# Retention's output matrix in column-block pairs, with four weight quads of each pair as seven block products

## The reference, cut to what matters

```python
y = (normalised_heads * silu(g)).reshape(B, S, R_HEADS * R_V_DIM) @ ret_w_out
x = layer_norm(ALPHA * x + y, ln_gain[i], ln_bias[i])
```

## Time and profile before

| | |
|---|---|
| median of 3 runs | 2163.74 us (2163.69 to 2163.83) |
| the profiled execution | 2162.95 us |
| its span, first to last instruction | 2161.2 us |
| TensorE busy | 2148.4 us, 99% of the span |
| VectorE busy | 1515.6 us, 70% |
| ScalarE busy | 1083.5 us, 50% |
| mean granted TensorE clock | 0.999 of full speed |

### The profile page before, as it was taken

One profiled execution on the slowest core, in us unless ns is written; L12 is line 12 of the kernel. 1 busy time (PEld: TensorE's weight loads), 2 busy tenths in 40 slices (PEclk: granted clock), 3 DMA queues, 4 the chain that ended last, 5 costly groups with the idle time before them and its releaser, 6 DMA issues.

```text
span 2161.2 us, 26090 instructions
## 1 busy us (share of the span) xinstructions
PE 2148.4 (99%) x9858; PEld 1781.5 (82%) x9858; DVE 1515.6 (70%) x1875; ACT 1083.5 (50%) x1356; POOL 218.3 (10%) x376
## 2 busy tenths in 40 slices
PE   9999999999999999999999999999999999999998
PEld 7878888888888888888888888888888888888886
DVE  6676676688888886858566876686766666666556
ACT  6554664555555554535444455445545444444433
POOL 1013024000000001000011361010000000000000
PEclk9999999999999999999999999999999999999999
DMA  9568478667767767666766786766666666765853
GB/s 318 196 177 231 147 238 268 198 195 222 222 189 212 238 208 227 200 220 202 246 224 195 208 224 181 273 226 204 184 204 207 193 188 190 214 186 173 295 201 108
DMA packets 385195, 455.64 MB, mean 211 GB/s; under 512 B 172545, under 2 KB 207761, under 8 KB 383936
## 3 DMA queue, kind: packets, MB, share of 16 engines
q1 hardware_dynamic: 368368, 415.50, 61.7%
q0 software_dynamic: 16432, 38.44, 5.7%
q10 hardware_dynamic: 288, 0.27, 0.0%
HBM read 415.33 MB, written 8.39 MB: 196 GB/s over the span
## 4 chain that ended last, share of the span: by engine, by line
PE 99%; DVE 0%; DMA 0%; SPq 0%; ACT 0%; issue 0%
PE bank L540 22%; PE bank L542 22%; PE bank L541 22%; PE bank L2627 9%; PE bank L2629 9%; PE bank L2628 9%; PE bank L554 1%; PE bank L556 1%; PE bank L555 1%; PE bank L2762 1%; PE bank L2749 1%; PE bank L2456 0%; PE bank L2859 0%; PE bank L2858 0%; PE bank L2857 0%; PE bank L573 0%
## 5 line engine op out<-in xcount | busy, mean ns | idle before, releaser
L519 DVE TENSOR_TENSOR wlo<-raw,whi 128x1024 fp32r<-128x1024 f32 (+1 forms) x537 | 643.7, 1213 | 388.5 <-ACT whi L512 386.9
L512 ACT ACTIVATE whi<-raw 128x1024 fp32r<-128x1024 f32 (+1 forms) x537 | 555.7, 1051 | 446.2 <-PE bank L542 412.3
L540 PE MATMUL bank<-whi,T1H 128*128 128x512 f32 (+1 forms) x1524 | 597.6, 392 | 0.0
L542 PE MATMUL bank<-whi,T1L 128*128 128x512 f32 (+1 forms) x1524 | 590.6, 388 | 0.0
L541 PE MATMUL bank<-wlo,T1H 128*128 128x512 f32 (+1 forms) x1524 | 590.1, 387 | 0.0
L430 ACT ACTIVATE whi<-raw 128x1024 fp32r<-128x1024 f32 (+1 forms) x264 | 265.2, 1016 | 267.3 <-PE bank L2629 216.3
L435 DVE TENSOR_TENSOR wlo<-raw,whi 128x1024 fp32r<-128x1024 f32 (+1 forms) x264 | 301.5, 1166 | 97.5 <-ACT whi L430 94.0
L540 PEld LDWEIGHTS bank<-whi,T1H 128*128 128x128 f32 x1524 | 286.3, 188 | 59.7 <-DVE wlo L519 1.7
L542 PEld LDWEIGHTS bank<-whi,T1L 128*128 128x128 f32 x1524 | 286.1, 188 | 59.3
L541 PEld LDWEIGHTS bank<-wlo,T1H 128*128 128x128 f32 x1524 | 286.3, 188 | 56.6
L2627 PE MATMUL bank<-whi,T1H 128*128 128x512 f32 x486 | 189.1, 389 | 0.0
(11 more groups left out here) (474 smaller groups left out, 2599.9 us busy)
## 6 DMA issues: line engine op xcount, KB each, us to landing
raw<-in_ret_w_in SPq DMA_DIRECT2D x64, 1024.0 KB, 5.5
raw<-in_w_ffn_down SPq DMA_DIRECT2D x44, 1024.0 KB, 6.0
raw<-in_attn_w_in SPq DMA_DIRECT2D x40, 1024.0 KB, 5.5
raw<-in_w_in SPq DMA_DIRECT2D x39, 1024.0 KB, 5.3
raw<-in_w_ffn_gate SPq DMA_DIRECT2D x72, 512.0 KB, 4.0
raw<-in_w_ffn_up SPq DMA_DIRECT2D x72, 512.0 KB, 5.0
raw<-in_ret_w_in SPq DMA_DIRECT2D x64, 512.0 KB, 4.6
raw<-in_ret_w_out SPq DMA_DIRECT2D x32, 1024.0 KB, 5.2
```

Source lines behind the costliest of these rows:

```text
L512: eng.activation(hi_[:, s, :, :n], raw[:, c % RAWS, HALF * hf:HALF * (hf + 1), :n], ACT.Copy).then_inc(hi_ready, 1)
L519: eng.tensor_tensor(lo[:, s, :, :n], raw[:, c % RAWS, HALF * hf:HALF * (hf + 1), :n], hi_[:, s, :, :n].bitcast(F32), ALU.subtract).then_in ...
L540: eng.matmul(o, TH[:, kt, xs], hi_[:, s, t, :n], start=first and t == 0, stop=False)
L542: m = eng.matmul(o, TL[:, kt, xs], hi_[:, s, t, :n], start=False, stop=last and t == HALF - 1)
```

## The change

Phase `out3` takes the columns in two pairs of blocks over all eight banks. Chunks 0 and 1 stay plain (tiles 0 to 3 of blocks 0 and 1). Then come 14 quads of the first pair (chunks 2 to 15) and 8 quads of the second pair (chunks 16 to 23), in the order of `OUT3`. Quads 2 to 5 of each pair are sevens: they stand at chunks 6, 8, 10, 12 and at 18, 20, 22, 23. After them come four plain chunks of block 2 (24 to 27), and then four of block 3 (28 to 31), which are again done for j = 0 and then for j = 1. Block 3 has no other plain chunks. So block 2 is now finished only when the last eight halves begin.

```diff
+OUT3 = [[6, 7, 8, 9, 2, 10, 3, 11, 4, 12, 5, 13, 14, 15], [0, 1, 2, 6, 3, 7, 4, 5]]
+OSEV = (2, 3, 4, 5)
+O3 = 16
+OQ = [2, O3]
...
+    SHo = at("SHo", 64 * KB, [P, 4, len(OSEV), P], F32R)
+    Ao = at("Ao", 72 * KB, [P, 2 * len(OSEV), T])
+    Sfo = at("Sfo", 80 * KB, [P, 4, len(OSEV), P])
+    SLo = at("SLo", 80 * KB, [P, 4, len(OSEV), P], F32R)
+    FX = at("FX", 88 * KB, [P, 4, W])
...
+    def out3_own(sb):
+        return ((bank[4], bank[6]), (bank[5], bank[7])) if sb == 0 else ((bank[2], bank[3]), (bank[0], bank[1]))
+
+    def out3_shared(sb):
+        return [bank[4 * sb + n] for n in range(4)]
...
+        for c in range(32):
+            for n in range(pieces("out3", c)):
+                if n == 1 and c in (out3_last(0) + 2, out3_last(1) + 2):
+                    out3_first_shared(c // O3)
+                if c == 30 and n == 0:
+                    act.wait_ge(mm_done, piece("out3", out3_last(1), 3)[0] + 1)
+                if c < O3 + len(OUT3[1]):
+                    piece_hi(act, "out3", c, n)
+                else:
+                    split_hi(act, "out3", c, n)
...
-                if b == 0 and h == 10:
+                if (c, n) == (5, 0):
                     turned_hi(act, SQ["ret"] + RH - 1, T2dH[:, 4 * RH - 4:4 * RH, :], oTz, BY_SP["ret"] + RH)
+                    act.wait_ge(x_parts, 18)
+                    act.activation(SHo[:, :, :, :], Sfo[:, :, :, :], ACT.Copy).then_inc(x_parts, 1)
...
+        def out3_fold(sb):
+
+            n = fold_no(2 + sb)
+            if sb == 0:
+                dve.wait_ge(r_og, 2 * RH)
+            dve.wait_ge(mm_done, piece("out3", out3_last(sb), 3)[0] + 1)
+            fold_shared(dve, FX, out3_shared(sb), n)
+            dve.wait_ge(xr4_in[0], 16 * (sb + 1))
+            dve.wait_ge(xr4_in[1], 16 * (sb + 1))
+            dve.wait_ge(fold, n + 5)
+            for b, j, t, op in ((0, 0, 0, ADD), (0, 1, 2, SUB), (1, 0, 3, ADD), (1, 1, 1, ADD)):
+                cs = slice((2 * sb + b) * W, (2 * sb + b + 1) * W)
+                stt(X4[:, j, cs], xr4[:, b, j, :], ALPHA, FX[:, t, :], MUL, op).then_inc(fold, 1)
...
+        for c in range(32):
+            if c < O3 + len(OUT3[1]):
+                lower_parts(dve, "out3", c)
...
+            if c == 3:
+                block_done(dve, "ret", 23, RH // 2 - 1)
+                a_, z_ = 2 * OSEV[0], 2 * OSEV[-1] + 2
+                tt(Ao[:, :, :], T2dH[:, a_:z_, :].bitcast(F32), T2dL[:, a_:z_, :].bitcast(F32), ADD).then_inc(x_parts, 1)
+                dve.wait_ge(x_parts, 14)
+                differences(dve, Sfo, *(Ao[:, k::2, j * P:(j + 1) * P] for j in range(J) for k in range(2)), x_parts, 14)
+            if c == 5:
+                turned_lo(dve, SQ["ret"] + RH - 1, T2dH[:, 4 * RH - 4:4 * RH, :], T2dL[:, 4 * RH - 4:4 * RH, :], oTz)
+                dve.wait_ge(x_parts, 19)
+                tt(SLo[:, :, :, :], Sfo[:, :, :, :], SHo[:, :, :, :].bitcast(F32), SUB).then_inc(x_parts, 1)
+            if c == out3_last(0) + 2:
+                out3_fold(0)
+            if c == O3 + 1:
+                dve.wait_ge(mm_done, halves(PLAN["out3"][0] + O3))
+                dve.wait_ge(fold, fold_no(2) + 9)
+                out3_sum(0)
+                out3_sum(1)
+            if c == O3 + 3:
+                out3_stats(0)
+                out3_stats(1)
+            if c == out3_last(1) + 3:
+                out3_fold(1)
+            if c == 29:
+                block_done(dve, "out3", 27)
+                dve.wait_ge(fold, fold_no(3) + 9)
+                out3_sum(2)
+                out3_stats(2)
...
+                if k in OSEV:
+                    if k == OSEV[0] and sb == 0:
+                        pe.wait_ge(acc_out[BLK["out3"] % 2], out3_free(-2))
+                        pe.wait_ge(acc_out[(BLK["out3"] + 1) % 2], out3_free(-1))
+                        pe.wait_ge(x_parts, 20)
...
+                    seven_of("out3", c, out3_own(sb), out3_shared(sb), T2dH, T2dL, SHo, SLo, k, k - OSEV[0], k == OSEV[0], k == OSEV[-1])
```

More of the change, by code:

```diff
@@ L98 @@
 DSEV = 4
+OUT3 = [[6, 7, 8, 9, 2, 10, 3, 11, 4, 12, 5, 13, 14, 15], [0, 1, 2, 6, 3, 7, 4, 5]]
+OSEV = (2, 3, 4, 5)
+O3 = 16
+OQ = [2, O3]
 SEVENS = ([PLAN["ffs"][0] + 8 * f + p for f in range(NSUM) for p in SEVEN]
-          + [PLAN["down"][0] + c for c, k in enumerate(DOWN[0] + DOWN[1]) if k < DSEV])
+          + [PLAN["down"][0] + c for c, k in enumerate(DOWN[0] + DOWN[1]) if k < DSEV]
+          + [PLAN["out3"][0] + OQ[sb] + n for sb in range(2) for n, k in enumerate(OUT3[sb]) if k in OSEV])
 def sevens(g):
@@ L855, in _ @@
                     block_across(sp, SQ["ret"] + RH - 1, oSz, oTz, r)
-            load(sp, "out3", c, [(0, W, chunk(A["ret_w_out_2"][0], c % 8, c // 8 * W))])
+            w = A["ret_w_out_2"][0]
+            if c < 2:
+                load(sp, "out3", c, [(0, W, chunk(w, 0, c * W))])
+            elif c < O3 + len(OUT3[1]):
+                sb = c // O3
+                k = OUT3[sb][c - OQ[sb]]
+                two_blocks_of(sp, "out3", c, w[2 * P * k:2 * P * k + 2 * P, 2 * W * sb:2 * W * sb + 2 * W].rearrange("(a p) n -> p a n", p=P))
+            else:
+                load(sp, "out3", c, [(0, W, chunk(w, 4 + c % 4, (c // 4 - 4) * W))])
         n = 0
@@ L1518, in _, with out3_first_shared @@
         last = RH // 2
[L1519 to L1522, removed]
+        def out3_first_shared(sb):
+            act.wait_ge(mm_done, piece("out3", out3_last(sb), 1)[0] + 1)
+            act.activation(FX[:, 0, :], out3_shared(sb)[0], ACT.Copy).then_inc(fold, 1)
+        for c in range(32):
[6 more added lines that the diff above has]
+                    piece_hi(act, "out3", c, n)
+                else:
+                    split_hi(act, "out3", c, n)
+                if (c, n) == (0, 0):
                     rstd(brs, r_ms, RH, r_rs)
                     table_silu()
-                if b == 0 and h == 3:
+                if (c, n) == (1, 1):
                     block_done(act, "ret", 23, last - 1)
@@ L2345, in _ @@
             assert rc_.n == RET[1], rc_.n
[L2347 to L2367, removed]
@@ new lines, in out3_sum, with out3_stats @@
+        def out3_sum(b):
+            banks = out3_own(b // 2)[b % 2]
+            for j in range(J):
+                d = X4[:, j, b * W:(b + 1) * W]
+                tt(d, banks[j], d, ADD).then_inc(acc_out[(BLK["out3"] + b) % 2], 1)
+        def out3_stats(b):
+            dve.wait_ge(acc_out[(BLK["out3"] + b) % 2], out3_free(b))
+            for j in range(J):
+                c = 6 * (FB * j + b)
+                ch.link(dve.bn_stats(bst[:, c:c + 6], X4[:, j, b * W:(b + 1) * W]))
+        for c in range(32):
+            if c < O3 + len(OUT3[1]):
+                lower_parts(dve, "out3", c)
+            else:
+                split_lo(dve, "out3", c, 0)
+                split_lo(dve, "out3", c, 1)
+            if c == 0:
+                dve.wait_ge(r_rs, RH)
+                for j in range(J):
+                    ts(oR[:, j, :], bank[(7, 5)[j]], bag[:, 2 * j:2 * j + 1], brs[:, j:j + 1], SUB, MUL).then_inc(r_norm, 1)
+            if c == 2:
+                B = BLK["out3"] - 1
+                dve.wait_ge(r_norm, 2 * RH)
+                dve.wait_ge(acc_out[B % 2], 2 * (B // 2) + 2)
+                for j in range(J):
+                    tt(oR[:, j, :], oR[:, j, :], gR[:, j, :], MUL).then_inc(r_og, 1)
+                for j in range(J):
+                    dve.wait_ge(r_og, 2 * RH - 1 + j)
+                    dve.transpose(oSz[:, j, :], oR[:, j, :]).then_inc(sq_dve, 1)
+            if c == 3:
[22 more added lines that the diff above has]
+                block_done(dve, "out3", 27)
+                dve.wait_ge(fold, fold_no(3) + 9)
+                out3_sum(2)
+                out3_stats(2)
@@ L2863, in _ @@
             ret(i, False)
[L2864 to L2872, removed]
+        pe.wait_ge(sq_dve, 3 * (SQ["ret"] + RH - 1))
+        for c in range(2):
+            if c:
+                pe.wait_ge(r_norm, 2 * RH)
+            for n in range(2):
+                q, slot, _, _ = piece("out3", c, n)
+                pe.wait_ge(lo_ready, q + 1)
+                for t in range(HALF):
+                    for j in range(J):
+                        m = three(out3_own(0)[c][j], T2dH, T2dL, x_of(2 * n + t, j), slot, t, n == 0 and t == 0, False)
+                m.then_inc(mm_done, 1)
+        for sb in range(2):
+            if sb:
+                pe.wait_ge(fold, fold_no(2) + 5)
+            for n, k in enumerate(OUT3[sb]):
+                c = OQ[sb] + n
+                if k in OSEV:
[3 more added lines that the diff above has]
+                        pe.wait_ge(x_parts, 20)
+                    if k == OSEV[0] and sb == 1:
+                        for b in range(2):
+                            pe.wait_ge(acc_out[(BLK["out3"] + b) % 2], out3_free(b))
+                    seven_of("out3", c, out3_own(sb), out3_shared(sb), T2dH, T2dL, SHo, SLo, k, k - OSEV[0], k == OSEV[0], k == OSEV[-1])
+                else:
```

(5 more changed lines are left out.)

9 lines of the change are left out of this document (8 added, 1 removed).

## The result

The changed kernel takes 2166.67 us (median of 20 runs, 2164.8 to 2167.72), the kernel before 2163.61 us in the same comparison. The ratio is 1.0013, with a 95% interval of 1.0007 to 1.0019: 0.13% slower, against the 2166.0 us that were forecast. The profiled execution took 2166.34 us.

The account below looks back on a forecast made before the run. TensorE, busy for 99% of the span, was taken as the bound. Stalls of 7.8 us against 5.44 saved made +2.4 us; the forecast was 2166.0 us (+0.1%), range 2162.7 to 2169.0.

Parts of the forecast that it names:

- The gain: Phase `out3`: eight sevens save 3 matmuls each, 24 steps of 0.2267 us, 5.44 us.
- What a seven asks of DVE, and the lead it needs: At every seven: about 7 us of DVE against TensorE's 4.76; entered 3.5 us ahead it barely stalls, each microsecond less costs one.
- the ledger: Whole phase: count of when DVE delivers each lower part and when TensorE wants it; stalls sum to 7.8 us.
- Rival 4: Weight loads in this phase land late because sevens hold their slot longer; 2167 to 2171 us, chance 4%.
- Chunk 6: First seven: DVE late behind transfers, `SHo` and `SLo`; stalls of 0.95 us at piece 0 and 2.43 at piece 2.
- Chunks 20 and 23, the last eight halves: Stalls of 1.50 us (statistics before the seven), 1.75 (two sevens side by side), 1.19 (block 2's sums and statistics).
- The sum: Whole kernel: 7.8 us of stalls against 5.44 saved, +2.4 us, giving 2166.0 us.
- rival 3: Clock falls to 1.2 GHz at a stall, costing 2 us; one to three falls give 2168 to 2172 us, chance 9%.
- The rival on the other side: Phase `out3`: DVE is never late, stalls under 1.1 us; 2158.6 us, chance 5%.

Follow-up runs that it names:

- experiment 7: Changed kernel with turned tiles later, `SHo` early, statistics behind chunk 24, block 2's sums and statistics behind chunk 31, chunk 23 plain (seven sevens); 2158.07 us.
- Experiments 2: Changed kernel with the four statistics of blocks 0 and 1 moved on DVE from behind chunk 19 to behind chunk 24; 2164.56 us.
- 3: Changed kernel with quad 5 of the second pair, at chunk 23, made plain again (24 matmuls instead of 21); 2165.11 us.
- 4: Changed kernel with block 2's two sums and two statistics moved on DVE from behind chunk 29 to behind chunk 31; 2164.98 us.
- 6: Changed kernel with four more statistics (2.9 us of DVE) added behind chunk 19 as a dose; 2170.70 us.
- experiments 1: Changed kernel with ACT's copy `SHo` put ahead of the wait for the last head's turned tiles; 2163.23 us.
- 5: Changed kernel with `SHo` early, `turned_hi` moved to the end of chunk 7 and `turned_lo` behind chunk 9; 2162.27 us.
- 10: As experiment 7, but with ACT's and DVE's order at chunks 5 to 9 as in the changed kernel; 2162.39 us.

## Why the prediction was right

**The gain**: 24 steps of 0.2267 us. Right; experiment 7 shows 21 of them to 0.01 us, 4.76 us. The Trainium skill, page "TensorE: Matmul & The Clock Gate", section "Back-to-back issue gap", gives N/2.4 + 2.5 ns for a matmul's gap taken by itself; by it the 21 would be 4.5 us, an estimate that the trace does not bear out.

**What a seven asks of DVE, and the lead it needs**: right, and the core of the case. Down's one gap of 0.25 us was enough to scale the ledger by. All five gaps stand where they were put and nowhere else, and chunks 8, 10, 12 and 18 have none. Rival 4 did not come: in the changed trace ACT never waits for a load of `ret_w_out` in this phase.

**Chunk 6**: the place and the order of steps are right, the first term was too large. It was to be 0.95 and was 0.46, because the whole phase began 0.16 us later and the turned tiles came at 1999.96, not 2000.3: the transposes did end later (1985.72 + 1.30 = 1987.02 against 1986.81), but the 16 transfers behind them did not. Over the profiles that left this order alone the first gap varies from 0.08 to 0.65 us.

**Chunks 20 and 23, the last eight halves**: 1.50, 1.75 and 1.19 forecast; 1.50, 1.76 and 1.16 measured in the profiled execution. Experiments 2, 3 and 4 remove each by its named cause, and 6 makes the gap at chunk 20 larger by nearly the dose.

**The sum**: five gaps 7.2 us (7.8 forecast), which alone would have given +1.8. What lifted it is rival 3, which got 9%: the clock fell in the profiled execution, where 1.8 + 1.7 makes 3.5 and 3.4 was measured. By the medians it is +3.06, and those of experiments 1, 5 and 10 point to a fall in most of the other executions, without showing it. Its price was about right (2 us forecast, 1.7 measured; the 0.43 us a step, which the earlier trace rows do not show as such, is in the changed trace). The step that failed is the argument against it: that the clock stayed full for 4.2 us after the last matmul does not show that 2.2 us of idling is safe. The forecast came out near because a term 0.6 too large and a term left out went in opposite directions; that part of it is luck.

**The rival on the other side** (DVE never late, 2158.6) was wrong for this order of work. Experiment 7, with the order changed and one seven fewer, has no gap and takes 2158.07.

## What to carry to other kernels

Where one engine is busy for 99%, arithmetic taken from it is worth its full time only if the engines that feed it can deliver at each place and not on average. Write down, for each unit of work that asks more of its feeder than it takes, how far ahead the feeder enters it, and move everything else out of the line just ahead of it (one copy placed behind a wait instead of before it cost 3.0 us here by the medians, 1.8 of it as gaps). And do not put two such units side by side without counting; one plain unit in place of the second was worth more here than the products that the second saved.

## What the hardware showed that was not expected

The clock fell to its lower level behind a gap of 2.2 us in a stage where TensorE was otherwise always busy: in the profiles of the changed kernel and of experiments 2 and 3 at chunk 6, of 6 at chunk 20 (gaps of 1.89 and 2.27 us with 2.2 us of work between), each time for 3.4 us. A gap of the same size left it full in the profiles of 4 and 10, and at chunk 6 in that of 6. So of seven gaps of 2.2 us or more in this phase four were followed by a fall. No gap of 1.65 us or less was, and no fall came in this phase without such a gap. At this size of gap it falls in some executions and not in others; what decides it stays open. The Trainium skill, page "TensorE: Matmul & The Clock Gate", section "What's actually happening", ties the lower level to an idle array, and the traces agree in direction. That a stall as short as this one could bring a fall is the forecast's own step and does not stand in that section; it rests on the four falls here.

After each wait TensorE's next step takes 0.31 to 0.34 us instead of 0.23 (2009.65 to 2009.96, 2014.01 to 2014.35), and more where the clock falls in it: about 0.1 us a stall on top of the gap, for gaps from 0.14 us to 2.2 us alike.
